# Mixture-of-experts stage of a fused transformer layer: its extra token blocks folded into two loops per expert, four weight buffers in place of three, another order of the weight transfers

## The chip, the cores and the metric

The kernel runs on one core of a Trainium2 chip. Its time is the device time of one execution in microseconds (us). The median of three runs of the kernel before is 1521.79 us (1521.5 to 1522.17). One more execution was profiled. A change under 0.2% of the time (3 us) counts as no change.

The engines are TensorE (PE, matmul), VectorE (DVE), ScalarE (ACT), GpSimd (POOL) and SyncE (SP, which here only issues transfers). Each runs its own instruction stream in order. They meet in semaphores.

## The reference

One layer for 256 prompt tokens and 64 sample tokens (T = 320), model width 2048: RMSNorm, attention and a gated convolution, output projection, and then the part that the change touches, a mixture of 32 experts with two experts per token. All in float32. Cut to what matters:

```python
gate = (g_p * top_p / sum(top_p))                     # weight of each of a token's 2 experts
expert_idx = g_idx[:, None] * 8 + top_i               # 4 groups of 8 experts
# for every expert e, on the rows xb of the tokens that chose it:
hb = silu(xb @ w_gate[e]) * (xb @ w_up[e])            # w_gate, w_up: 2048 x 512
y  = (hb @ w_down[e]) * gate                          # w_down: 512 x 2048
h  = h + segment_sum(y)                               # back to the tokens
y_prompt, y_sample = rmsnorm(h)
```

Each of the three matrices of an expert has 4 MB (4.19 million bytes), and all 32 experts are read whatever the routing is, 403 million bytes.

## The kernel before, in words

Up to about 545 us the kernel computes norms, projections, attention and the output projection with its router logits. The expert stage follows, and then a final norm of about 20 us.

**Blocks.** The tokens of an expert are handled in blocks of B = 32. With 320 tokens and two choices each, an expert has 20 tokens on average, and in these inputs one expert of the 32 has more than 32, so 33 blocks are computed: 31 experts have one block, and expert 19 has two. A table in SBUF (`tables`) holds the counts, computed by DVE, and the engines read it into registers.

**One block on PE.** `gather` picks the tokens' rows out of the normalised activations by matmul (L841); ACT copies them, `gathered_T` transposes them (L847), and ACT copies again to `xg`. `gate_or_up` multiplies by the gate matrix and then by the up matrix (L864, 16 matmuls of 32 rows each, which the profile shows as 32 records), ACT copies each result (L1191), `fold` sums four partial sums and transposes (L870). ACT computes silu (L1194), DVE multiplies (L1564) into `hT`. `down` multiplies by the down matrix (L879), ACT copies `yb` (L1234), and `combine` spreads the block's rows back over the tokens in 12 matmuls (L890), each of which DVE adds to `hreg` (L1561). `gates_T` (L852) prepares the weights that combine uses. The gather for the next expert is done between this expert's gate and up.

**PSUM banks.** combine writes its 12 pieces to the eight banks in the order `COMB_BANKS`, and an engine that wants a bank waits on `comb_added` until the addition that frees it is done. The gate result goes to bank 2, which the sixth addition frees before the change.

**Blocks beyond the first.** Expert 19's second block is `extra_blocks(e)`, a branch with its own buffers (`xx`, `hTx`, `gTx`, `yx`), which PE enters after the first block's gate and up and before its down: it computes gate and up once more with the same matrices, then down and combine, and then PE goes back for the first block's down.

**Transfers.** The weights lie in three slots of 32 KB per partition (the six 16 KB parts of `ring`): gate, up, down. SP loads expert e's gate when the gate matrix of e-1 is used, then its up, then its down (L482), each as one transfer of 4 MB, and where expert e-1 has extra blocks it waits for these as well (`extra_used`). The transfers of expert 0 are issued at the end of the output projection (L474, six of 2 MB). The gain of the final norm is loaded by POOL at `hg_ready` (1 MB).

**Names for the steps below.** U(e) is the moment at which PE is done with the up matrix of expert e-1, so that up(e) can be issued. D(e) is the start of expert e's first `down`.

## Time and profile before

| | |
|---|---|
| median of three runs | 1521.79 us |
| profiled execution, its own time | 1520.95 us |
| its span, first to last instruction | 1518.7 us |
| PE busy | 1343.1 us (88%) |
| DVE busy | 596.3 us (39%) |
| ACT busy | 347.2 us (23%) |
| granted TensorE clock, mean | 0.925 |
| moved by DMA | 473.91 MB, mean 312 GB/s |
| share of the chain that ended last: PE / DMA | 52% / 41% |

The span is 2.25 us shorter than the time of the same execution. A busy share is an average over stages with different limits: in the 40 slices of the profile the DMA engines are busy 9 tenths in nearly every slice from the 17th on, and 0 to 6 tenths in most of the slices before, while PE is busy 7 to 9 tenths in all but the first. The granted clock is in tenths of full speed (2.4 GHz), and its lower level is half of that. "Idle before, releaser" in a row is how long the engine stood still ahead of the instruction, and what released it.

### The profile page before, as it was taken

How to read it: one execution, taken by the hardware profiler on the slowest of the kernel's cores; microseconds unless marked ns; L12 is line 12 of the kernel's file. 1: busy time of each engine (PE TensorE's matmuls, PEld its weight loads, DVE VectorE, ACT ScalarE, POOL GpSimd, SP SyncE). 2: the span in 40 equal slices, each digit the busy share in tenths (PEclk: the TensorE clock that was granted, in tenths of full speed). 3: DMA queues.
4: the chain of work that ended last, by engine and by line, in shares of the span. 5: the costliest groups of instructions: out<-in, count | busy, mean ns of one | idle time of the engine just before them, and what ended most of it. 6: DMA issues, size and time to landing. Idle time of an engine off the chain costs nothing.

```text
span 1518.7 us, 22119 instructions
## 1 busy us (share of the span) xinstructions
PE 1343.1 (88%) x8510; PEld 714.1 (47%) x8511; DVE 596.3 (39%) x1183; ACT 347.2 (23%) x591; POOL 32.0 (2%) x41
## 2 busy tenths in 40 slices
PE   5999999999999999788888888888889988887885
PEld 4989999566666663232222322322323322223221
DVE  6335444044574443242243234224324422332344
ACT  5332322123453322111111111111211111111113
POOL 1000000000000000000000000000000000000000
PEclk9999999999999989999898888988989989889887
DMA  9454451023353368999999999999989999999994
GB/s 323 132 166 137 161 167 60 10 70 111 92 180 112 132 284 358 411 434 433 430 430 435 432 430 432 434 431 430 433 362 397 432 434 431 432 432 433 431 432 180
DMA packets 69607, 473.91 MB, mean 312 GB/s; under 512 B 9516, under 2 KB 46512, under 8 KB 55680
## 3 DMA queue, kind: packets, MB, share of 16 engines
q1 hardware_dynamic: 68640, 470.85, 76.0%
q0 software_dynamic: 832, 2.48, 0.5%
q8 instruction: 29, 0.48, 0.1%
q14 instruction: 10, 0.08, 0.0%
q10 hardware_dynamic: 96, 0.02, 0.0%
HBM read 469.97 MB, written 3.38 MB: 312 GB/s over the span
## 4 chain that ended last, share of the span: by engine, by line
PE 52%; DMA 41%; DVE 3%; issue 2%; ACT 1%; SPq 0%; DVEq 0%; ACTq 0%
DMA ring<-in_w_down 41%; PE ps L879 11%; PE ps L579 5%; PE ps L580 5%; PE ps L581 5%; PE ps L864 3%; PE ps L640 2%; PE ps L667 2%; PE ps L730 2%; PE ps L731 2%; PE ps L732 2%; PE ps L743 2%; PE ps L841 2%; PE ps L661 1%; PE ps L870 1%
## 5 line engine op out<-in xcount | busy, mean ns | idle before, releaser
L1561 DVE TENSOR_TENSOR hreg<-ps,hreg 128x512 f32<-128x512 f32 (+1 forms) x396 | 239.6, 679 | 290.2 <-PE ps L890 290.2
L864 PE MATMUL ps<-ring,mix 128*32 128x512 f32 x2112 | 281.6, 681 | 30.4 <-DMA ring<-in_w_up 17.9
L879 PE MATMUL ps<-ring,mix 128*32 128x512 f32 x1056 | 166.2, 787 | 60.6 <-DMA ring<-in_w_down 53.1
L890 PE MATMUL ps<-mix 32*128 32x512 f32 (+1 forms) x792 | 156.3, 612 | 26.4 <-ACT mix L1234 25.6
L1191 ACT COPY mix<-ps 128x512 f32<-128x512 f32 x66 | 70.5, 1069 | 448.3 <-PE ps L864 448.3
L864 PEld LDWEIGHTS ps<-ring,mix 128*32 128x32 f32 x2112 | 74.6, 122 | 207.8 <-issue 177.8
L579 PE MATMUL ps<-xT_hi,w_hi 128*128 128x320 f32 (+1 forms) x528 | 165.5, 313 | 4.9 <-DVE w_lo L1299 2.9
L580 PE MATMUL ps<-xT_lo,w_hi 128*128 128x320 f32 (+1 forms) x528 | 164.5, 312 | 0.0
L581 PE MATMUL ps<-xT_hi,w_lo 128*128 128x320 f32 (+1 forms) x528 | 164.4, 311 | 0.0
L1299 DVE TENSOR_TENSOR w_lo<-ring,w_hi 128x1024 fp32r<-128x1024 f32 (+1 forms) x66 | 76.7, 1205 | 105.9 <-ACT w_hi L1006 105.9
L879 PEld LDWEIGHTS ps<-ring,mix 128*32 128x32 f32 x1056 | 40.0, 138 | 160.7 <-issue 103.9
L890 PEld LDWEIGHTS ps<-mix 32*128 32x128 f32 (+1 forms) x792 | 51.3, 166 | 133.7 <-issue 68.0
L579 PEld LDWEIGHTS ps<-xT_hi,w_hi 128*128 128x128 f32 (+1 forms) x528 | 99.4, 188 | 6.2 <-issue 3.6
L841 PE MATMUL ps<-r,work 128*32 128x512 f32 (+1 forms) x840 | 101.8, 595 | 0.0
L580 PEld LDWEIGHTS ps<-xT_lo,w_hi 128*128 128x128 f32 (+1 forms) x528 | 99.6, 189 | 0.3
L581 PEld LDWEIGHTS ps<-xT_hi,w_lo 128*128 128x128 f32 (+1 forms) x528 | 99.5, 188 | 0.2
L1006 ACT CAST w_hi<-ring 128x1024 fp32r<-128x1024 f32 (+1 forms) x66 | 65.0, 1033 | 149.2 <-PE ps L581 149.2
L1564 DVE TENSOR_TENSOR mix<-mix,ps 128x128 f32<-128x128 f32 x33 | 9.5, 288 | 226.3 <-PE ps L870 216.3
L870 PEld LDWEIGHTS ps<-const,mix 128*128 128x128 f32 x528 | 63.8, 191 | 53.5 <-issue 27.7
L870 PE MATMUL ps<-const,mix 128*128 128x32 f32 x528 | 71.0, 279 | 18.2 <-ACT mix L1191 18.2
L1234 ACT COPY mix<-ps 128x512 f32<-128x512 f32 x32 | 18.8, 586 | 215.8 <-PE ps L879 215.8
L841 PEld LDWEIGHTS ps<-r,work 128*32 128x32 f32 (+1 forms) x840 | 25.6, 108 | 69.4 <-issue 68.6
(259 smaller groups left out, 1187.5 us busy)
## 6 DMA issues: line engine op xcount, KB each, us to landing
ring<-in_w_gate SPq DMA_DIRECT2D x31, 4096.0 KB, 22.1
ring<-in_w_up SPq DMA_DIRECT2D x31, 4096.0 KB, 23.7
ring<-in_w_down SPq DMA_DIRECT2D x31, 4096.0 KB, 23.7
ring<-in_w_in SPq DMA_DIRECT2D x32, 1024.0 KB, 8.2
ring<-in_w_o SPq DMA_DIRECT2D x16, 1024.0 KB, 6.8
hreg<-in_x_prompt SPq DMA_DIRECT2D x4, 1024.0 KB, 6.2
ring<-in_w_up SPq DMA_DIRECT2D x2, 2048.0 KB, 11.6
ring<-in_w_gate SPq DMA_DIRECT2D x2, 2048.0 KB, 8.2
```

Source lines behind the costliest of these rows:

```text
L579: pe.matmul(out, hi, xT_hi[:, c, :], start=c == 0, stop=False)
L580: pe.matmul(out, hi, xT_lo[:, c, :], start=False, stop=False)
L581: last = pe.matmul(out, lo, xT_hi[:, c, :], start=False, stop=c == KC - 1)
L841: last = pe.matmul(ps[B * j:B * (j + 1), bank, :], pk[0:tn, i, :], xn[0:tn, i, 4 * j:4 * j + 4, :].rearrange("t c q -> t (c q)"), start=i ...
L864: last = pe.matmul(ps[r:r + B, bank, :], x[:, k % 4, k // 4, :], w[:, k, :], start=k < 4, stop=k >= KC - 4)
L870: last = pe.matmul(ps[:, 3, 64 * c + B * m:64 * c + B * m + B], hsb[m][:, c, :], const[:, C_FOLD:C_FOLD + B], start=True, stop=True)
L879: last = pe.matmul(ps[B * j:B * (j + 1), 4, :], h[:, c, :], w[:, c, 512 * j:512 * j + 512], start=c == 0, stop=c == 3)
L890: pe.matmul(ps[0:tn, COMB_BANKS[u % 8], :], gates[r, t0:t0 + tn], rows[r, :], start=True, stop=True).then_inc(full_sem, 1)
L1006: act.copy(w_hi[:, u % 2, 8 * half:8 * half + 8, 0:width], w_raw(u, half)).then_inc(w_hi_ready, 1)
L1191: act.copy(hsb[m].rearrange("p c q -> p q c"), ps[:, bank, :].rearrange("p (q c) -> p q c", c=4)).then_inc(signal, 1)
L1299: dve.tensor_tensor(w_lo[:, u % 2, f, 0:width], w_raw(u, half), w_hi[:, u % 2, f, 0:width].bitcast(F32), ALU.subtract).then_inc(w_lo_ready, 1)
L1561: dve.tensor_tensor(h, ps[0:tn, COMB_BANKS[u % 8], :], h, ALU.add).then_inc(signal, 1)
```

## The change

1. The separate code for extra blocks is gone. For each expert PE, ACT and DVE run two loops over its blocks: the first does gate and up of every block and keeps the products in `hTs` (one place per block), the second does down and combine of every block. Before each down ACT copies the block's product from `hTs` to `hT`.
2. `gate_b`, a fourth slot of 32 KB per partition, is laid over `mix` and its neighbours, whose contents are no longer needed. Even experts take their gate matrix from the ring, odd ones from `gate_b`. Gate 1 is loaded as soon as `hg_ready` is 12.
3. SP issues, in this order: up(e) after U(e), gate(e+1), down(e). For the last two experts it is up, down, gate, up, down, and the last down comes in four pieces of 1 MB with a semaphore each.
4. A block's gates transpose waits for 5 additions of the block before it in the second loop, and its down for 6; `COMB_BANKS` is reordered. The gate matmuls wait for the seventh addition of the preceding expert's last block instead of the sixth.
5. In a block, `fold(1)` now comes ahead of `gathered_T`.
6. The gain of the final norm is loaded after the last down matrix, into the ring. The router matrix goes to `krt` and is loaded after the residual input.

The core of the diff (buffers that only move, and the semaphores' declarations, are left out):

```diff
-COMB_BANKS = (5, 6, 7, 1, 4, 2, 0, 3)
+COMB_BANKS = (5, 6, 7, 1, 0, 4, 2, 3)
...
-            sp.wait_ge(routed, 4)
-            with sp.Fori(1, NE) as e:
-                used = sp.value_load(tables[0:1, 3, bass.ds(e, 1)], min_val=1, max_val=65)
-                for m in range(3):
-                    sp.wait_ge(weights_used, e * 3 + (m + 1 - 3))
-                    sp.wait_ge(extra_used[m], used)
-                    w = a[("w_gate", "w_up", "w_down")[m]][0, bass.ds(e, 1)].rearrange("a b c -> (a b) c")
-                    sp.dma_start(ring[:, 2 * m:2 * m + 2, :].rearrange("p s n -> p (s n)"), rows_of(m, w)).then_inc(slot_full[2 * m], 16)
+            sp.wait_ge(hg_ready, 12)
+            sp.dma_start(gate_b[:, :], rows_of(0, a["w_gate"][0, 1])).then_inc(gate_b_full, 16)
+            sp.wait_ge(routed, 2)
...
+            def load_gate(e, before, dst, signal):
+                sp.wait_ge(gate_done, before)
+                sp.dma_start(dst, expert_rows("w_gate", 0, e)).then_inc(signal, 16)
+
+            def load_up(e, before):
+                sp.wait_ge(up_done, before)
...
+            before = blocks_before(1)
+            load_gate(2, before, gate_a, slot_full[0])
+            load_up(1, before)
+            load_down(1, before)
+            with sp.Fori(2, NE - 3, 2) as e:
+                before = blocks_before(e)
+                load_up(e, before)
+                load_gate(e + 1, before, gate_b[:, :], gate_b_full)
+                load_down(e, before)
+                before = blocks_before(e + 1)
+                load_up(e + 1, before)
+                load_gate(e + 2, before, gate_a, slot_full[0])
+                load_down(e + 1, before)
+
+            before = blocks_before(NE - 2)
+            load_up(NE - 2, before)
+            load_down(NE - 2, before)
+            load_gate(NE - 1, before, gate_b[:, :], gate_b_full)
+            before = blocks_before(NE - 1)
+            load_up(NE - 1, before)
+            sp.wait_ge(down_done, before)
+            for c in range(4):
+                sp.dma_start(ring[:, 4 + c // 2, D * (c % 2):D * (c % 2 + 1)],
+                             rows_of(2, a["w_down"][0, NE - 1])[:, D * c:D * (c + 1)]).then_inc(down_last[c - 1] if c else slot_full[4], 16)
...
+            def expert(e, odd):
+                first = pe.value_load(tables[0:1, 0, bass.ds(e, 1)], min_val=0, max_val=NE + 20)
+                count = pe.value_load(tables[0:1, 1, bass.ds(e, 1)], min_val=1, max_val=MAXB)
+                with pe.Fori(0, count) as k:
+                    it = first + k
+                    pe.wait_ge(xg_ready, it + 1)
+                    pe.wait_ge(comb_added, first * 12 + 7)
+                    gate_full(e, odd)
+                    gate_or_up(xg, 0, odd, 2).then_inc(gate_done, 1)
+                    pe.wait_ge(comb_added, first * 12 + 8)
+                    pe.wait_ge(pick_ready, it + 2)
+                    gather(pickr, 0, gathered)
+                    pe.wait_ge(h_copied, it * 2 + 1)
+                    pe.wait_ge(hT_ready, it + 1)
+                    fold(0).then_inc(folded, 1)
+                    matrix_full(1, e)
+                    gate_or_up(xg, 1, odd, 4).then_inc(up_done, 1)
+                    pe.wait_ge(h_copied, it * 2 + 2)
+                    pe.wait_ge(silu_ready, it + 1)
+                    fold(1).then_inc(folded, 1)
+                    pe.wait_ge(g_copied, it + 2)
+                    pe.wait_ge(comb_added, first * 12 + 12)
+                    gathered_T(gsb, 1, transposed)
+                tail = pe.value_load(tables[0:1, 2, bass.ds(e, 1)], min_val=0, max_val=16)
+                after = first + count
+                with pe.Fori(0, count) as k:
+                    it = first + k
+                    pe.wait_ge(hT_ready, after + 1)
+                    pe.wait_ge(comb_added, it * 12 + 5)
+                    pe.wait_ge(gates_ready, it + 1)
+                    gates_T(gpick, gt_full)
+                    pe.wait_ge(comb_added, it * 12 + 6)
+                    pe.wait_ge(h_picked, it + 1)
+                    down(hT, e, tail + 1).then_inc(down_done, 1)
+                    pe.wait_ge(xg_ready, after + 1)
+                    pe.wait_ge(gt_copied, it + 1)
+                    pe.wait_ge(y_copied, it + 1)
+                    pe.wait_ge(comb_added, it * 12 + 12)
+                    combine(gT, yb, comb_full, comb_added, it * 12 + 12)
...
+            with act.Fori(0, NE) as e:
...
+                after = first + count
+                with act.Fori(0, count) as k:
+                    it = first + k
+                    act.wait_ge(hT_ready, after + 1)
+                    act.copy(hT, hTs[:, bass.ds(k, 1), :].rearrange("p b q -> p (b q)")).then_inc(h_picked, 1)
...
-            pool.wait_ge(hg_ready, 12)
-            pool.dma_start(gain, a["norm_final"].rearrange("(a d) -> a d", a=1).to_broadcast([P, D])).then_inc(s_gfin, 16)
+            pool.wait_ge(down_last[2], 17)
+            pool.dma_start(gain_last, a["norm_final"].rearrange("(a d) -> a d", a=1).to_broadcast([P, D])).then_inc(s_gfin, 16)
```

How the instructions stand in a row. First SP, whose rows are the transfers, from the last of expert 0's to the loop over the experts. In the kernel before:

```order
L474 DMA ring<-in_w_down 128x4096 [waits psum_full] x2
L476 UNCONDITIONAL_BRANCH [waits routed]
L476 ISA
L477 TENSOR_LOAD tables
L477 ISA x2
L479 ISA
L482 ISA [waits extra_used0,weights_used]
L482 DMA ring<-in_w_gate 128x8192
L479 REGISTER_ALU
L482 DMA ring<-in_w_up 128x8192 [waits extra_used1,weights_used]
L482 DMA ring<-in_w_down 128x8192 [waits extra_used2,weights_used]
```

The same place in the changed kernel, to the end of the loop's first expert:

```order
L471 DMA ring<-in_w_down 128x4096 [waits psum_full] x2
L473 DMA gate_b<-in_w_gate 128x8192 [waits hg_ready]
L492 TENSOR_LOAD tables [waits routed]
L492 ISA x2
L481 DMA ring<-in_w_gate 128x8192 [waits gate_done]
L485 DMA ring<-in_w_up 128x8192 [waits up_done]
L489 DMA ring<-in_w_down 128x8192 [waits down_done]
...
L485 DMA ring<-in_w_up 128x8192 [waits up_done]
L481 ISA [waits gate_done]
L481 DMA gate_b<-in_w_gate 128x8192
L489 DMA ring<-in_w_down 128x8192 [waits down_done]
```

Gate 1 has moved ahead of the wait for the routing, and in the loop the up transfer, which waits for `up_done`, stands ahead of the next gate.

PE from the end of the up matmuls to the first down matmul, in the kernel before (L864 up, L847 gathered_T, L870 fold, L852 gates_T, L879 down; the part of the extra blocks, which is jumped over, is left out):

```order
L864 MATMUL ps<-ring,mix 32x512 x15
L944 REGISTER_ALU [waits g_copied]
L847 MATMUL ps<-const,mix 128x128 [waits comb_added]
L847 MATMUL ps<-const,mix 128x128 x3
L948 REGISTER_ALU
L870 MATMUL ps<-const,mix 128x32 [waits h_copied]
L870 MATMUL ps<-const,mix 128x32 x3
L852 MATMUL ps<-const,work 128x128 [waits gates_ready]
...
L895 COMPARE_AND_BRANCH
...
L879 MATMUL ps<-ring,mix 32x512 [waits slot_full5,slot_full4]
```

And in the changed kernel (L911 up, L917 fold, L884 gathered_T, L889 gates_T, L930 down):

```order
L911 MATMUL ps<-ring,cq 32x512 x15
L961 REGISTER_ALU
L917 MATMUL ps<-const 128x32 [waits silu_ready,h_copied]
L917 MATMUL ps<-const 128x32 x3
L965 REGISTER_ALU [waits g_copied]
L884 MATMUL ps<-const,work 128x128 [waits comb_added]
...
L947 COMPARE_AND_BRANCH
...
L889 MATMUL ps<-const,work 128x128 [waits gates_ready]
...
L900 ISA [waits h_picked,comb_added]
L930 MATMUL ps<-ring,work 32x512 [waits slot_full5,slot_full4]
```

The transposes of the gathered rows stood in the time in which ACT copies the up result, and now stand behind the fold; a loop's end and the next loop's start lie between them and gates_T, and down has a new wait, `h_picked`, for ACT's copy.

ACT in its first loop over the blocks, changed kernel (L1212 copy of the gate or up result, L1205 copy of the gathered rows, L1215 silu):

```order
L1223 ISA
L1212 ACT_TABLE_LOAD
L1212 COPY work<-ps 128x128x4 [waits gate_done]
L1204 REGISTER_ALU
L1205 COPY work<-ps 128x512 [waits gathered]
L1228 ISA
L1215 ACT_TABLE_LOAD
L1215 ACTIVATE work<-ps 128x128 [waits folded]
L1212 COPY const<-ps 128x128x4 [waits up_done]
```

Two loads of activation tables now stand inside the loop. Before, expert 0 was written out ahead of the loop with the only such load of the stage, and the loop had none.

## Rows read from the trace of the kernel before

**Rows 1.** Stretches of time: engines' busy us (instructions), granted clock, DMA share, GB/s.
```profile
567.00:575.00 8.00, 6.57 (x60) 2.17 (x52) 5.22 (x19) 1.17 (x2) 0.00 (x0) 1.00 0.17 49
575.00:668.00 93.00, 78.67 (x596) 29.69 (x592) 30.91 (x68) 19.55 (x30) 0.00 (x0) 0.94 0.99 416
668.00:1105.00 437.00, 367.97 (x2505) 126.23 (x2505) 147.90 (x315) 66.60 (x105) 0.00 (x0) 0.88 1.00 432
1131.00:1137.00 6.00, 5.54 (x51) 2.36 (x54) 1.33 (x5) 1.10 (x3) 0.00 (x0) 1.00 0.12 49
```
**Rows 2.** Timeline of PE, expert 2's down to expert 3's: start, us, what.
```profile
643.54 3.64 PE L879 MATMUL ps<-ring,mix 128*32 128x512 f32 x32
647.97 4.74 PE L890 MATMUL ps<-mix 32*128 32x512 f32 x24 [0.79 <-ACT mix L1234]
653.03 3.64 PE L864 MATMUL ps<-ring,mix 128*32 128x512 f32 x32 [0.32 <-DVE hreg L1561]
656.46 2.92 PE L841 MATMUL ps<-r,work 128*32 128x512 f32 x24
659.31 1.08 PE L870 MATMUL ps<-const,mix 128*128 128x32 f32 x8
660.32 3.64 PE L864 MATMUL ps<-ring,mix 128*32 128x512 f32 x32
663.89 0.66 PE L847 MATMUL ps<-const,mix 128*128 128x128 f32 x4
665.11 1.08 PE L870 MATMUL ps<-const,mix 128*128 128x32 f32 x8 [0.56 <-ACT mix L1191]
668.01 3.64 PE L879 MATMUL ps<-ring,mix 128*32 128x512 f32 x32 [1.37 <-DMA ring<-in_w_down]
```
**Rows 3.** Two later downs after a longer and a shorter wait.
```profile
1404.83 6.42 PE L879 MATMUL ps<-ring,mix 128*32 128x512 f32 x32 [3.38 <-DMA ring<-in_w_down]
1433.98 5.34 PE L879 MATMUL ps<-ring,mix 128*32 128x512 f32 x32 [1.54 <-DMA ring<-in_w_down]
```
**Rows 4.** Transfers whose issue ended a stretch without transfers (SP's timeline).
```profile
573.56 0.35 SPq L482 DMA_DIRECT2D ring<-in_w_gate  x1
1136.64 0.34 SPq L482 DMA_DIRECT2D ring<-in_w_gate  x1
```
**Rows 5.** One up transfer of 2 MB alone, window 505 to 520: KB, us to landing.
```profile
ring<-in_w_up SPq DMA_DIRECT2D x1, 2048.0 KB, 7.6
```
**Rows 6.** Downs of experts 18, 19 (its second block, then its first) and 22.
```profile
1105.12 6.09 PE L879 MATMUL ps<-ring,mix 128*32 128x512 f32 x32 [3.39 <-DMA ring<-in_w_down]
1145.41 3.64 PE L879 MATMUL ps<-ring,mix 128*32 128x512 f32 x32
1154.54 3.64 PE L879 MATMUL ps<-ring,mix 128*32 128x512 f32 x32
1229.99 3.64 PE L879 MATMUL ps<-ring,mix 128*32 128x512 f32 x32 [0.48 <-DMA ring<-in_w_down]
```
**Rows 7.** Around expert 0's gate: transposes, ACT's copy, gate.
```profile
568.35 0.66 PE L847 MATMUL ps<-const,mix 128*128 128x128 f32 x4 [0.71 <-ACT mix L1184]
569.04 0.59 ACT L1188 COPY mix<-ps 128x512 f32<-128x512 f32 x1 [0.75 <-PE ps L847]
569.73 3.64 PE L864 MATMUL ps<-ring,mix 128*32 128x512 f32 x32 [0.72 <-issue]
```
**Rows 8.** The gain of the final norm, in the page's list of transfers.
```profile
ckv<-in_norm_final POOLq DMA_DIRECT2D x1, 1024.0 KB, 11.9
```
**Rows 9.** ACT: the one table load of the stage, and silu in a later expert.
```profile
581.04 1.28 ACT L1194 ACT_TABLE_LOAD   x1
606.22 0.28 ACT L1194 ACTIVATE mix<-ps 128x128 f32<-128x128 f32 x1 [0.39 <-PE ps L870]
```
**Rows 10.** The last down, and the first use of the final gain.
```profile
1492.24 5.34 PE L879 MATMUL ps<-ring,mix 128*32 128x512 f32 x32 [1.66 <-DMA ring<-in_w_down]
1506.87 2.35 DVE L1656 SCALAR_TENSOR_TENSOR hreg<-hreg,small,ckv 128x2048 f32<-128x2048 f32 x1
```

More of the change, by code:

```diff
@@ L423, in late_loads @@
             sp.wait_ge(psum_full, full(f"K{H - 1}_1"))
+            sp.dma_start(gain, a["norm_ffn"].to_broadcast([P, D])).then_inc(s_gffn, 16)
+            sp.wait_ge(psum_full, full(f"PV{H - 1}"))
+            sp.wait_ge(s_stage, 64)
+            sp.wait_ge(ssq_full, 4)
+            for i, (t0, tn) in enumerate(TILES):
+                sp.dma_start(xtile[0:tn, i, :], x_src[i]).then_inc(s_xagain, 16)
             sp.dma_start(wr[:, :, 0:G], a["w_router_group"][0].rearrange("(c p) e -> p c e", p=P)).then_inc(s_router, 16)
@@ L965, in _ @@
+            for c in range(3):
+                pe.sem_inc(down_last[c], 1)
             keep_clock(3, 5)
```

345 lines of the change are left out of this document (124 added, 221 removed).

## The prediction

> **What bounds the kernel now.** I read the stretches of time first. From 668 to 1105 us the transfers run at 432 GB/s with the DMA engines' share at 1.00 [rows 1]: 15 experts in 437.1 us from expert 3's down to expert 18's [rows 2, 6], so 29.14 us per expert of three matrices, 9.71 us per matrix. There the stream of weights is the bound and nothing in this change makes it faster. The change can win only where the stream stands still, and after its end. The stretches show two such places: 567 to 575 us (49 GB/s, so 7.1 of 8 us idle) with the 93 us behind it (416 GB/s, 3.4 us idle), and 1131 to 1137 us (49 GB/s) at expert 19, the one with two blocks. For the second place the downs give the sum: from expert 18's to expert 22's, 124.87 us where four experts of 29.14 would be 116.56, so 8.3 us lost [rows 6].
>
> The timeline of PE then says how close PE is to being the bound. Where it does not wait, down to the end of up takes 4.43 (down, and ACT's copy) + 5.06 (combine, held by DVE's additions) + 3.43 (gate) + 2.85 (gather) + 1.01 (fold) + 3.57 (up) = 20.35 us, and the next down could start 2.8 us later (668.01 less its wait of 1.37, from 663.89) [rows 2]: 23.2 us, 5.9 less than the stream needs. After a wait PE is slower: the granted clock is 0.88 in the long stretch against 1.00 where PE does not wait [rows 1], and a down that takes 3.64 us takes 5.34 behind a wait of 1.54 and 6.42 behind one of 3.38 [rows 2, 3]. I take +1.7.
>
> From issue to landing a transfer costs more than its bytes. 2 MB alone took 7.6 us [rows 5], of which 4.85 are bytes at 432 GB/s, so 2.75 are not. At expert 19 the stream was empty some 2.4 us before the landing that the downs imply (1105.12 + 29.14 = 1134.3, against a stretch that is all but empty from 1131 [rows 1]), and 573.56 was followed by traffic at about 574.8 [rows 1, 4]. I take 1.0 from issue to the first byte and 2.4 from the last byte to landing, 3.4 together; bounds 2.7 and 3.7. The Trainium skill (DMA: Bandwidth & Descriptors, Anatomy of one DMA) puts the fixed cost of a DMA at about 2.0 us, most of it the receipt of the last byte. The trace shows more here; by 2.0 each of the three gaps below would be 1.4 shorter, 4 us in all, as an estimate.
>
> **PE's cycle after the change.** Gate waits for the seventh addition, not the sixth: 7.26/12 = 0.61 us more (DVE adds one piece per 0.61; combine to gate was 5.06 = six of them and the start). The time from down to the end of up is 20.96. Behind up, the fold starts 1.22 us later as before and occupies PE for 0.92 (1.08 with its end); the transposes, which stood in ACT's shadow [rows 2], now follow; transposes to the end of ACT's copy is 1.28 [rows 7]; then the new copy of hT on ACT, which no row shows. Its bounds are 0 (hidden) and the 0.59 of a copy four times as wide [rows 7]; silu on the same 128 columns takes 0.28 [rows 9], and I take 0.3. With 0.4 for semaphores and the entry to the second loop that is 4.1 in place of 2.8. The loop entry's bounds are 0 and the 0.72 that expert 0's gate waited for issue [rows 7]. So the cycle is **25.1 us**, range 24.5 to 26.5. That still fits into 29.14, but 2.3 us more of it lie on a path that decides at the places below.
>
> Is the stream still full in between? Put expert e-1's landed down at 0. The stream holds up(e), gate(e+1), down(e) and is empty at 29.1 - 2.4 = 26.7. The next up is issued at 20.96 + 1.7 = 22.7, first byte 23.7. The margin is 3.0 us, or 1.3 if the gate is slow as well. Full, at a cost of 0; if it is not, see the rivals.
>
> **The start.** The final gain (1 MB, 2.4 us of stream) leaves it: -2.4 [rows 8]. Gate 1 goes into it before the routing, 9.7 us. The stream was empty at 567, and would now be at 567 - 2.4 + 9.7 = 574.3; gate 2 is issued when expert 0's gate is done, as the gate of expert 1 was (573.56) [rows 4], so a gap of 0.5 to 0.8. Then gate 2, up 1, down 1: full to 603.9. U(2) is expert 0's end of up, 569.73 + 3.43 + 2.85 + 1.0 + 3.57 = 580.6, plus 25.1: 605.7, first byte 606.9 with the 1.2 seen here. A gap of 3.0. Together 3.8 against 7.1 + 3.4 = 10.5 before: **-6.7**, with the gain -9.1. The routing's shorter chain on DVE gains nothing (PE was still busy with its filler matmuls), and the later router load has 10 us to spare.
>
> **Expert 19.** Expert 18's down landed at 0. U(20) comes only when both blocks are done with up, and gate 21 stands behind it in SP's row. First block: end of up at 22.7. Second: fold 1.22 + 0.92, transposes to gate 1.38, gate 3.43, gather 2.85, fold 1.01, up 3.57 = 14.4 [rows 2, 7]. So U(20) = 37.1, first byte 38.1, against an empty stream at 26.7: a gap of 11.4. Then it is full to 38.1 + 29.1 = 67.2, as down 20 is issued in time: the first down at 41.2, the second 9.7 later (9.13 between the two before [rows 6], and a gates transpose), its end 54.5. The wait for five and six additions costs nothing, since four are past when combine ends and DVE needs 0.61 for each of the rest, but it does not shorten anything either. U(21) = 50.9 + 20.96 = 71.8, first byte 72.8: a second gap of 5.6. Before, the extra block's gate was used first and freed its slot at 1136.64, 31.5 us after the landing [rows 4, 6], and the gate led the queue. So 17.0 against 8.3: **+8.7**.
>
> **The end.** The last matrix would land at 1492.24 - 9.1 + 8.7 = 1491.8. But now PE is late. With expert 28's down landed at 0, eight transfers end at 77.7; D(29) = 29.1, D(30) = 29.1 + 25.1 + 1.7 = 55.9, D(31) = 81.0. So the last down starts **3.3** behind the last landing, and the four pieces overlap nothing. Because PE has not waited it is fast, 3.64 and not 5.34: **-1.7**. The final gain is loaded behind the last piece; it needs 11.9 us at worst [rows 8] and is used 14.6 - 1.7 + 3.3 = 16 us after it [rows 10]: hidden, 0.
>
> **ACT's tables.** Two loads per block, 33 blocks, 1.28 us each [rows 9]: 85 us more on ACT. The one ahead of the gate's copy runs while PE does combine. The one ahead of silu starts at about 605.8 in the terms of the rows (silu at 606.22 now), so silu ends near 607.4, and the fold that waits for it comes 4.8 us after 606.1, at 610.9. Cost 0. The Trainium skill (ScalarE: Activation LUTs, What ACT_TABLE_LOAD costs) counts 2.66 us for a switch, with a drain of 1.38 behind the 1.28. The trace shows silu 0.02 behind the load; by the page the rival with exposed tables below would cost 88 us and not 42, and its chance stays small because even 2.66 would fit under this cover.
>
> **Sum.** -2.4 - 6.7 + 8.7 + 3.3 - 1.7 = +1.2 us on the span of 1518.7: 1519.9. The profiled execution took 2.25 more than its span, 1522.2, and it lies 0.8 under the median of the runs, so **1523.0**.
>
> **Rivals.** *PE's cycle is longer (slower).* The places are U(2), U(20), U(21), D(30) and D(31): one extra us in the cycle makes the gaps 1, 1 and 2 us longer and the end 2, so 6 us per us. At 26.5, the top of my range, it is +8.4 and 1531. It decides from a cycle of 25.4 on, where the sum passes +3. For it: the new copy, two loop entries and the register loads all stand between the fold and down. Against: in the loop before, the jump over the extra part did not show. A variant is a stream that empties every time: if U comes 1 us after the margin of 3.0, each expert costs 0.5 us, since the same delay is spread over two, and 31 of them 15: about 1538. It needs a cycle beyond 28 or a slow down and a slow gate at once. *Tables exposed (slower):* if each block's load delayed a copy that PE waits for, 33 x 1.28 = 42 us, but only where PE's path decides; for all, 1565. ACT's idle time of 3 to 9 us before these copies speaks against it.
>
> *A shorter cycle (faster).* At 24.3 (the hT copy and the loop entry hidden, the transposes not) it is -4.8: 1518.2. *The double expert costs what it did (faster).* If the second gap of 5.6 is not there, because PE is ahead by more than I count, 1517.4; with the first gap short too, 1514.3. That needs expert 19 to start before its down of 18 landed, which the row of SP doesn't allow. *The change does only what the start shows:* with the double expert and the end as before, 1523.0 - 8.7 - 3.3 + 1.7 = 1512.7; I see no reason for that in the rows, but it is the lower bound.
>
> **How the numbers follow.** Chances: forecast within 3 us (which is 0.2%, what a measurement can tell) 0.38; longer cycle 0.25, a stream that empties 0.06, tables 0.03, so slower 0.34; shorter cycle 0.15, the double expert 0.10, only the start 0.03, so faster 0.28. The cycle's range of 24.5 to 26.5 alone gives 1519.4 to 1531.4; the latency's bounds of 2.7 to 3.7 move the gaps' sum by -2 to +1, and whether downs and gates are slow or fast at experts 19 and 29 by 3 either way. The range is 1514 to 1532; the forecast's own is 1520 to 1526.
>
> **What would show it.** Per expert 29.14 us between landed downs in the long stretch, at 432 GB/s. Gate 1's transfer issued near 545.5, no stretch of 7 us without traffic at 567. A stretch without traffic of some 11 us after expert 18's down, and one of 5 to 6 about 30 us later. Gate 5.67 us after combine's start, down about 4.1 after the end of up where nothing else is late. A last down without a DMA wait ahead of it, 3.64 us long. I am wrong if the stream stays full at expert 19, or if it shows gaps at every expert.

## The result, and the profile after the change

| | before | after |
|---|---|---|
| median | 1521.64 us (1521.5 to 1522.17, 4 runs) | 1539.57 us (1536.62 to 1542.97, 4 runs) |
| profiled execution: time / span | 1520.95 / 1518.7 us | 1537.64 / 1535.8 us |

The ratio after/before is 1.0119, 95% interval 1.0105 to 1.0132: slower by 18 us, 16.6 above the forecast of 1523.0 and 7.6 above the range's upper end. The page of the kernel after: busy time, and the chain that ended last.

```profile
PE 1322.5 (86%) x8482; PEld 703.6 (46%) x8483; DVE 597.9 (39%) x1176; ACT 440.1 (29%) x687; POOL 31.9 (2%) x41
PE 57%; DMA 34%; DVE 3%; issue 3%; ACT 2%; DVEq 0%; SPq 0%; ACTq 0%
```

The share of DMA in the chain fell from 41% to 34% and PE's rose from 52% to 57%: PE decides more of the time. Stretches of the kernel after, against [rows 1] (columns as there):

```profile
567.00:575.00 8.00, 6.27 (x44) 2.37 (x48) 1.44 (x4) 2.19 (x3) 0.00 (x0) 0.79 0.78 334
604.00:609.00 5.00, 4.84 (x44) 1.91 (x40) 0.00 (x0) 2.24 (x4) 0.00 (x0) 1.00 0.29 121
670.00:1105.00 435.00, 354.36 (x2490) 120.83 (x2490) 146.47 (x306) 107.86 (x146) 0.00 (x0) 0.90 1.00 429
1138.00:1152.00 14.00, 13.06 (x100) 4.15 (x98) 1.24 (x5) 5.14 (x7) 0.00 (x0) 0.88 0.00 0
1182.00:1190.00 8.00, 7.14 (x64) 2.51 (x56) 0.00 (x0) 3.95 (x5) 0.00 (x0) 1.00 0.04 16
```

Each gap is where it was forecast, and each is larger. The old one at 567 has shrunk (334 GB/s in place of 49), but 573 to 575 still carries only 25 GB/s: gate 2 waits for expert 0's gate, which took 5.34 and not the 3.64 of [rows 7] (the window, and the gate on PE's timeline):

```profile
573.00:575.00 2.00, 2.00 (x24) 0.86 (x20) 0.00 (x0) 0.32 (x1) 0.00 (x0) 0.93 0.08 25
569.29 5.34 PE L911 MATMUL ps<-ring,cq 128*32 128x512 f32 x32 [1.73 <-issue]
```

The new one at 604 cost 5.1 us where 3.0 were forecast (3.6 of them in this window, by its 121 GB/s against 432, the rest until up 2's first byte behind it). Behind expert 18 nothing moves for 14 us (11.4 forecast), and 30 us later for 8 more (5.6 forecast). In the last three gaps PE is over 85% busy: the transfers wait for PE.

SP's timeline of the kernel after shows what ended the gaps, against [rows 4], where it was a gate:

```profile
609.05 0.35 SPq L485 DMA_DIRECT2D ring<-in_w_up  x1
609.61 0.34 SPq L481 DMA_DIRECT2D gate_b<-in_w_gate  x1
1152.11 0.33 SPq L485 DMA_DIRECT2D ring<-in_w_up  x1
1152.64 0.33 SPq L481 DMA_DIRECT2D gate_b<-in_w_gate  x1
1189.20 0.34 SPq L485 DMA_DIRECT2D ring<-in_w_up  x1
```

An up ends each of these three gaps, and 0.5 us behind it comes a gate whose slot had long been free: it stood in SP's row behind the up that waited.

PE's timeline over one cycle of the kernel after, from expert 0's down to expert 1's, in which PE waits for no transfer, against [rows 2]:

```profile
585.77 3.64 PE L930 MATMUL ps<-ring,work 128*32 128x512 f32 x32 [0.30 <-ACT work L1237]
590.30 4.76 PE L941 MATMUL ps<-krt,const 32*128 32x512 f32 x24 [0.88 <-ACT krt L1241]
596.22 5.34 PE L911 MATMUL ps<-gate_b,cq 128*32 128x512 f32 x32 [1.16 <-DVE hreg L1564]
601.37 2.90 PE L878 MATMUL ps<-r,work 128*32 128x512 f32 x24
604.19 1.08 PE L917 MATMUL ps<-const,work 128*128 128x32 f32 x8
605.20 3.64 PE L911 MATMUL ps<-ring,cq 128*32 128x512 f32 x32
609.99 1.08 PE L917 MATMUL ps<-const 128*128 128x32 f32 x8 [1.15 <-ACT const L1212]
610.90 0.64 PE L884 MATMUL ps<-const,work 128*128 128x128 f32 x4
611.76 0.64 PE L889 MATMUL ps<-const,work 128*128 128x128 f32 x3 [0.23 <-DVE work L1568]
612.71 3.64 PE L930 MATMUL ps<-ring,work 128*32 128x512 f32 x32 [0.31 <-ACT work L1237]
```

The cycle is 26.9 us, not 25.1. The way from the end of up (608.8) to down is 3.9, as forecast (4.1). Combine to gate is 5.9 (forecast 5.67), but the gate takes 5.34 where I had 3.64 from [rows 2]; over the next such gate, from 623.58 to 628.95, the granted clock is 0.68. PE stood idle for 1.16 ahead of it, and not 0.32 as there. For even experts combine to gate is 6.34 with 1.58 idle, and the cycle 27.4 to 27.9 where no transfer is waited for.

Three of the periods between downs are 31.3 us and not 29.14, two in the long stretch (from 669.96 and 963.44) and one from 1396.86. The first of them on PE's timeline:

```profile
669.96 6.46 PE L930 MATMUL ps<-ring,work 128*32 128x512 f32 x32 [2.59 <-DMA ring<-in_w_down]
683.67 6.43 PE L911 MATMUL ps<-ring,cq 128*32 128x512 f32 x32 [1.58 <-DVE hreg L1564]
693.75 3.64 PE L911 MATMUL ps<-ring,cq 128*32 128x512 f32 x32
701.25 3.64 PE L930 MATMUL ps<-ring,work 128*32 128x512 f32 x32 [0.30 <-ACT work L1237]
```

Down and gate both run slow, up ends at 697.4, which is 27.4 behind the landed down, and the stream is empty at 26.7 by the forecast's own working: the "slow down and slow gate at once" of the rival of a stream that empties. The end, PE, POOL and DVE, against [rows 10]:

```profile
1494.41 5.34 PE L911 MATMUL ps<-gate_b,cq 128*32 128x512 f32 x32 [1.07 <-DVE hreg L1564]
1510.90 3.64 PE L930 MATMUL ps<-ring,work 128*32 128x512 f32 x32 [0.30 <-ACT work L1237]
1505.18 0.60 POOL L580 DMA_DIRECT2D ring<-in_norm_final  x1 [1084.61 <-DMA ring<-in_w_down]
1523.93 2.35 DVE L1635 SCALAR_TENSOR_TENSOR hreg<-hreg,small,ring 128x2048 f32<-128x2048 f32 x1
```

The last piece landed at 1505.18 (POOL was released then), the last down started 5.7 behind it (3.3 forecast) and took 3.64 as forecast. The final gain is used 18.7 us after its issue: hidden.

The profiled executions by segments, the times of expert n's down being D(n); a loss is the segment less 29.14 us per expert. The kernels to the right are experiments below.

| | before | after | e2 | e9 | e10 | e11 |
|---|---|---|---|---|---|---|
| D(3) at | 668.0 | 670.0 | 667.3 | 675.7 | 670.5 | 672.1 |
| lost D(3) to D(18) | 0.0 | 3.2 | 0.2 | 2.2 | -0.7 | -3.5 |
| lost D(18) to D(22), with expert 19 | 8.3 | 23.3 | 18.5 | 16.5 | 18.2 | 10.0 |
| lost D(22) to D(29) | 0.0 | 2.1 | -2.6 | 0.8 | -10.5 | -10.8 |
| D(29) to D(31) | 58.3 | 54.8 | 54.2 | 52.2 | 54.1 | 56.1 |
| D(31) to the end | 26.5 | 24.9 | 24.9 | 26.6 | 24.9 | 26.6 |

In e10 and e11 down 29 stands ahead of gate 30 in the queue, which alone takes 9.7 off the fourth line.

Against the forecast, after is +1.4 at D(3) (668.0 - 9.1 and one more matrix ahead of it, 9.7, is 668.6), +3.2 in the long stretch, +6.3 at expert 19, +2.1 behind expert 22, +2.9 from D(29) to D(31) (51.9 forecast) and +0.1 behind it: 16.0, and 1519.9 + 16.0 = 1535.9 for a span of 1535.8.

### The profile page after: what moved, and what is told of

Its sections match the earlier page's. It is cut to its first block, busy times and chain, and to the rows that moved or that the text cites. A ratio compares the mean times of both kernels' runs of the same rounds, so it can differ in the third digit from the quotient of the medians.

```text
span 1535.8 us, 23172 instructions
## 1 busy us (share of the span) xinstructions
PE 1322.5 (86%) x8482; PEld 703.6 (46%) x8483; DVE 597.9 (39%) x1176; ACT 440.1 (29%) x687; POOL 31.9 (2%) x41
## 4 chain that ended last, share of the span: by engine, by line
PE 57%; DMA 34%; DVE 3%; issue 3%; ACT 2%; DVEq 0%; SPq 0%; ACTq 0%
DMA ring<-in_w_down 33%; PE ps L930 11%; PE ps L911 7%; PE ps L615 5%; PE ps L616 5%; PE ps L617 5%; PE ps L878 2%; PE ps L676 2%; PE ps L703 2%; PE ps L766 2%; PE ps L767 2%; PE ps L768 2%; PE ps L779 2%; PE ps L917 2%; DVE hreg L1564 1%
## 5 line engine op out<-in xcount | busy, mean ns | idle before, releaser
L911 PE MATMUL ps<-ring,cq 128*32 128x512 f32 x1568 | 195.4, 642 | 25.3 <-DVE hreg L1564 23.5
L930 PE MATMUL ps<-ring,work 128*32 128x512 f32 x1056 | 163.6, 776 | 51.6 <-DMA ring<-in_w_down 48.6
L941 PE MATMUL ps<-krt,const 32*128 32x512 f32 (+1 forms) x792 | 157.0, 613 | 29.5 <-ACT krt L1241 29.5
L911 PEld LDWEIGHTS ps<-ring,cq 128*32 128x32 f32 x1568 | 53.3, 116 | 137.0 <-issue 135.3
L941 PEld LDWEIGHTS ps<-krt,const 32*128 32x128 f32 (+1 forms) x792 | 48.9, 166 | 140.3 <-issue 75.5
L1212 ACT COPY work<-ps 128x512 f32<-128x512 f32 x33 | 36.1, 1093 | 269.0 <-PE ps L911 269.0
L930 PEld LDWEIGHTS ps<-ring,work 128*32 128x32 f32 x1056 | 40.1, 137 | 147.9 <-issue 95.8
L911 PE MATMUL ps<-gate_b,cq 128*32 128x512 f32 x544 | 74.5, 697 | 18.2 <-DVE hreg L1564 17.3
L917 PE MATMUL ps<-const 128*128 128x32 f32 x264 | 35.6, 279 | 37.8 <-ACT const L1212 37.8
L917 PEld LDWEIGHTS ps<-const 128*128 128x128 f32 x264 | 31.9, 191 | 67.8 <-ACT const L1212 67.8
## 6 DMA issues: line engine op xcount, KB each, us to landing
ring<-in_w_down SPq DMA_DIRECT2D x30, 4096.0 KB, 23.3
ring<-in_w_gate SPq DMA_DIRECT2D x15, 4096.0 KB, 23.4
ring<-in_w_up SPq DMA_DIRECT2D x2, 2048.0 KB, 10.5
```

The lines of the kernel that those rows point to most:

```text
L911: last = pe.matmul(ps[r:r + B, bank, :], x[:, k % 4, k // 4, :], w[:, k, :], start=k < 4, stop=k >= KC - 4)
L917: last = pe.matmul(ps[:, 3, 64 * c + B * m:64 * c + B * m + B], hsb[m][:, c, :], const[:, C_FOLD:C_FOLD + B], start=True, stop=True)
L930: last = pe.matmul(ps[B * j:B * (j + 1), 4, :], h[:, B * c:B * (c + 1)], w[:, c, 512 * j:512 * j + 512], start=c == 0, stop=c == 3)
L941: pe.matmul(ps[0:tn, COMB_BANKS[u % 8], :], gates[r, t0:t0 + tn], rows[r, :], start=True, stop=True).then_inc(full_sem, 1)
L1212: act.copy(hsb[m].rearrange("p c q -> p q c"), ps[:, bank, :].rearrange("p (q c) -> p q c", c=4)).then_inc(signal, 1)
```

## The experiments

Theory A: PE's cycle is 27 to 28 us, and the places where the stream waits for PE turn that into time; SP's order (the free gate behind the waiting up) makes each place dearer. Rivals: the double expert alone; the seventh addition; the tables.

**e1, the gate needs only the fifth addition.** A cheaper cause of the idle time ahead of the gate.

```
-COMB_BANKS = (5, 6, 7, 1, 0, 4, 2, 3)      gate waits for comb_added first * 12 + 7
+COMB_BANKS = (5, 6, 7, 1, 2, 0, 4, 3)      gate waits for comb_added first * 12 + 5
```

(In exchange gates_T waits for the sixth addition and down for the seventh, one more each.)

> The changed kernel with another bank order: the gate result goes to the bank that the fifth addition frees, not the seventh, so gate follows combine after about 0.1 to 0.5 us and not 1.1 (1.6 in even experts). Theory A (PE's cycle decides at the start, at expert 19 and at the end, and the short idle ahead of gate costs the slow clock too: gate 5.34 instead of 3.64): cycle shorter by 0.6 to 1.0 for the wait and by up to 1.7 for the clock, six times: 1539.6 - 6 to - 14, so 1526 to 1534. Theory B (the loss is in the order of the transfers alone): 1537 or more.

Measured: 1541.27 us (1540.95 to 1544.21), ratio 1.0133 (1.0116 to 1.015). No gain; it was expected at 1526 to 1534. PE's timeline of e1 at the first such gate, and DVE's with the twelve additions before it:

```profile
599.86 5.34 PE L911 MATMUL ps<-gate_b,cq 128*32 128x512 f32 x32 [1.14 <-DVE hreg L1564]
595.12 7.26 DVE L1564 TENSOR_TENSOR hreg<-ps,hreg 128x512 f32<-128x512 f32 x12 [4.11 <-PE ps L941]
```

Five additions at 0.605 each end near 598.2, and gate starts 1.6 us later. The idle time is as long as with seven, though the profile still names DVE as releaser. With two additions less to wait for, nothing changed, so in this kernel the addition does not end the wait; something later does, which e7 looks for, and the releaser in the row is only the last semaphore that the view could name.

**e2, the next gate ahead of up in SP's loop.**

```
-                load_up(e, before)
                 load_gate(e + 1, before, gate_b[:, :], gate_b_full)
+                load_up(e, before)
```

(and so for the odd expert.)

> The changed kernel with SP's order next gate, up, down in the loop (the end of the program as it is). Theory A: the stream stands still at expert 19 because gate 21 is queued behind up 20; with gate 21 issued at the end of the second block's gate (7.7 us before its up) the gaps of 14.6 and 8 become together about 15, and the gap of 5 at 604 goes: about 12 us less, 1526 to 1530. Theory B (the stream's gaps are not what sets the end, PE's own cycle is): less than 4 us, 1536 or more.

Measured: 1523.57 us (1521.99 to 1524.74, 10 runs), ratio 1.0008 (0.9998 to 1.0018): 16 us less than after (12 expected), and no different from before. SP's timeline of e2 at the double expert:

```profile
1139.07 0.33 SPq L481 DMA_DIRECT2D gate_b<-in_w_gate  x1
1146.35 0.34 SPq L485 DMA_DIRECT2D ring<-in_w_up  x1
1163.48 0.33 SPq L489 DMA_DIRECT2D ring<-in_w_down  x1
```

The gate leads and fills the stream for 9.7 us while PE does gather and up. The table shows the gain in every segment but the last (3.0 in the long one, 4.8 at expert 19, 4.7 behind it); the gap at 604 is gone. PE's cycle is no shorter (26.9 from D(0) to D(1)): the order alone keeps the stream fed. Its largest cost left over before is still expert 19, 18.5 against 8.3, now in three gaps of 9, 4.5 and 3 us.

**e3 and e4, one block per expert, in after and in before.** One line on DVE sets the number of further blocks to zero.

```
             link(dve.tensor_reduce(extra, cmp, AX, ALU.add))
+            link(dve.tensor_scalar(extra, extra, 0.0, None, ALU.mult))
```

> The changed kernel without expert 19's second block (its tokens beyond 32 are added into another expert's rows). Theory A: the gaps at expert 19 cost 22.6 us here, so 1517 plus or minus 3, and the difference to the same edit in the kernel before is 2 to 6 us. Theory B (each expert costs more, everywhere): 1528 or more, difference 12 or more.

> The kernel before, also without expert 19's second block. Both theories: the 8.3 us that the downs of experts 18 to 22 show go, 1513 to 1514. It is the other half of the comparison with the one-block form of the changed kernel.

Measured: e3 1518.87 us (1512.8 to 1520.64, 10 runs), ratio 0.9973 (0.996 to 0.9986); e4 1514.93 us (1513.49 to 1516.35), ratio 0.9957 (0.994 to 0.9974). Both kernels leave out the second block. The double block costs 20.7 us in after and 6.7 in before: about 14 of the 18 us are made at expert 19, give or take 3 by the intervals; the table's 23.3 against 8.3 says 15. The remaining 4 are the long stretch, which shows in e3 as in after (3.15 lost from D(3) to D(18)), and the late end, less the start's gain.

**e5, the transposes ahead of the second fold again.**

```
+                    pe.wait_ge(g_copied, it + 2)
+                    pe.wait_ge(comb_added, first * 12 + 12)
+                    gathered_T(gsb, 1, transposed)
                     pe.wait_ge(h_copied, it * 2 + 2)
```

(and taken out behind the fold.)

> The kernel after, with PE's transposes of the gathered block (0.64 us) ahead of the second fold again, where they stood before, in the shadow of ACT's copy (fold idles 1.15 for it). Theory A (the loss is PE's own row of work, 6 us of time per us of its cycle): the way from the end of up to down goes from 4.0 to 3.5 (not more, since the gates' transposes and ACT's copy of hT then end at nearly the same time), so 0.4 to 0.5 per cycle, 2 to 4 us in all: 1535.5 to 1537.5 against 1539.6. Rival B (the order of the transfers alone sets the gaps, PE's cycle hardly counts): no change, 1539.6 within 1.5.

Measured: 1532.08 us median, but 1530.48 to 1541.86 over five runs; ratio 1.0069 (1.0049 to 1.009). Four runs lie within 2 us, 7 below after; the fifth is the profiled one, so its trace shows none of the gain: there expert 0's down took 5.34 instead of 3.64, and the gate behind it 6.48. It does show the way from the end of up to down, 3.5 in place of 3.9. A gain of 7 us is more than six times 0.4. Rival B is unlikely by the four runs, but no trace shows their gain; why they are so good is open.

**e6, no table loads in the loop.** One Silu on a spare column stands ahead of it.

```
+            act.activation(small[:, 63:64], eps_col, ACT.Silu)
             act.wait_ge(routed, 2)
```

> The kernel after with one Silu on a spare column ahead of ACT's loop, so that the loop needs no table loads (66 fewer, 85 us of ACT's time). Theory A (both loads of a block lie behind work of PE): no change, 1539.6 within 1.5. Rival T (the load ahead of silu or of the gate's copy delays a copy that PE waits for): up to 1.28 per cycle at the places where PE decides, 6 places at least: 1532 or less.

Measured: 1536.57 us (1531.63 to 1539.14), ratio 1.0092 (1.0065 to 1.012), which overlaps after's interval. PE's cycle is 26.90 from D(0) to D(1) against 26.94, and expert 19 costs 22.7 against 23.3. The loads are hidden, as forecast. ACT's timeline of the kernel after, against [rows 9]:

```profile
659.91 1.28 ACT L1215 ACT_TABLE_LOAD   x1
661.20 0.28 ACT L1215 ACTIVATE work<-ps 128x128 f32<-128x128 f32 x1
663.88 1.02 ACT L1212 COPY const<-ps 128x512 f32<-128x512 f32 x1 [2.41 <-PE ps L911]
```

Silu starts 0.01 behind the load, and ACT then has 2.4 us until up is done. The drain of 1.38 us that the Trainium skill (ScalarE: Activation LUTs, What ACT_TABLE_LOAD costs) adds to a load does not appear here.

**e7, e3 with straight code on PE.**

```
-                with pe.Fori(0, count) as k:
-                    it = first + k
+                first = it = e
```

(both loops; the loads of first and count go.)

> The kernel after with one block per expert as in e3 (the second block of expert 19 is left out and its tokens go to another expert's rows), and PE's two inner loops over blocks replaced by straight code for one block: no loads of first and count, no loop ends. To be compared with e3's 1518.9. Theory L (the idle time of 1.1 and 1.6 us between combine and gate is PE's sequencer at the loops' ends and register loads, and gate is slow, 5.34 for 3.64, because the clock falls in that idle time): idle before gate under 0.6 for odd experts, gate 3.5 to 3.8, cycle near 25, last down 3 to 4 behind the last landing in place of 5.7, gap at 604 near 3: 1512 to 1516. Rival S (the wait is for DVE's seventh addition, as the profile's releaser says, or for another engine's loop): idle unchanged, 1518.9 within 2.

Measured: 1507.96 us (1506.84 to 1512.12), ratio 0.9913 (0.9893 to 0.9933), below the 1512 to 1516 expected. Like e3 it leaves out the second block. PE's timeline of e7:

```profile
588.61 4.74 PE L941 MATMUL ps<-krt,const 32*128 32x512 f32 x24 [0.90 <-ACT krt L1236]
594.15 3.64 PE L911 MATMUL ps<-gate_b,cq 128*32 128x512 f32 x32 [0.80 <-DVE hreg L1559]
608.94 5.32 PE L930 MATMUL ps<-ring,work 128*32 128x512 f32 x32 [0.33 <-ACT work L1232]
```

Combine to gate is 5.54 (5.65 for even experts), idle 0.80 and 0.91, and the cycle from the down at 584.07 to that at 608.94 is 24.9. What is left of the idle time agrees with the seventh addition alone (0.32 before, plus 0.61): by DVE's timeline gate now starts 0.1 to 0.2 us behind the end of that addition, where in after it starts 0.4 behind it, 0.9 for even experts. With a fast gate the forecast's 25.1 holds. So the inner loop's end and its loads are worth 0.3 us, 0.7 with the outer loop's. The idle time was forecast under 0.6 and is 0.8, for which that addition is enough. The medians of e7 and e3 differ by 10.9 us, the profiled executions only by 3.0 (e7's is the slowest of its four), and all of it was made before D(0), at 584.07 against 587.07. From D(0) to D(3) e7 is 0.3 ahead, and behind it not at all. So the trace shows the shorter cycle, and no trace shows what the shorter cycle gained in time: the 10.9 us are not explained.

**e8, three fillers behind combine, and e12, one.**

```
                     combine(gT, yb, comb_full, comb_added, it * 12 + 12)
+                    pe.wait_ge(comb_added, it * 12 + 17)
+                    keep_clock(3, 0)
```

> The kernel after with a wait for the fifth addition behind combine and three filler matmuls (3 x 0.21 us, into the bank that it frees) at the end of PE's second loop, so that PE works while its sequencer goes through the loop's end. Theory C (gate is slow because the granted clock falls in the idle time, 0.68 in that stretch): gate 3.5 to 3.9 in the places where PE decides, cycle 1 to 1.6 shorter, 6 us per us: 1530 to 1535. Rival D (gate is slow for another reason, such as the transfers that write beside it; or the fall comes all the same, from the 0.6 of waiting ahead of the fillers): gate 5.3, the cycle the same or 0.3 longer, 1539 to 1542.

Measured: 1546.98 us (1542.41 to 1551.05), ratio 1.017 (1.0138 to 1.0202): 7 slower than after. PE's timeline of e8:

```profile
593.44 4.76 PE L941 MATMUL ps<-krt,const 32*128 32x512 f32 x24 [0.88 <-ACT krt L1243]
598.13 2.84 PE L855 MATMUL ps<-const 128*128 128x512 f32 x6
600.90 3.64 PE L911 MATMUL ps<-gate_b,cq 128*32 128x512 f32 x32
```

Theory C is right on the gate: with no idle time ahead of it, it takes 3.64 in all 31 cycles (14 of 31 take 5.00 or more in after). Part of the low clock comes back elsewhere: 23 of the 33 downs take 5.0 us or more, 17 in after. Summed up, what gates and ups take above 3.64 each falls from 29.7 us to 1.7, and what downs take above it rises from 43.5 to 51.4. And a filler takes 0.95 us, not the 0.21 that I wrote, so three of them use up what the clock gives back (cycle 26.8), and in the double expert they stand twice. One filler:

> e8 with one filler matmul in place of three. e8 showed the gates at 3.64 us, but its three fillers took 2.84 us, more than the idle time of 1.1 to 1.6 that they filled, and the double expert has them twice more. One takes 0.95. Theory C (the clock falls in the idle time at the loop's end): gate 3.64 in most places and cycle 25.9 to 26.6 in place of 26.9 to 28.1, so 1530 to 1536. Rival D (one filler of 0.95 with idle time on both sides holds no clock): gates 5.3 again, 1538 to 1543.

Measured: 1538.28 us (1533.87 to 1541.04), ratio 1.0105 (1.0073 to 1.0137). 3 of 31 gates are slow and the first cycle is 25.8, yet expert 19 costs 23.0, as in after, and the time moves by no more than the runs spread. Two of the three slow gates stand where PE decides (627.11, and expert 20's at 1180.09, 5.27), and the first down of expert 19 takes 5.16 there. Inconclusive as a remedy.

**e9, PE's first block straight, a loop only for more.**

```
+                one(first, first)
+                count = pe.value_load(tables[0:1, 1, bass.ds(e, 1)], min_val=1, max_val=MAXB)
+                with pe.If(count > 1):
+                    with pe.Fori(1, count) as k:
+                        one(first + k, first)
```

(`one` is the body of the first loop, `two` that of the second, treated alike.)

> The kernel after, all blocks computed, but PE's first block of an expert is straight code and a loop follows only where there are more (first is loaded once per pair of experts, count behind up). Theory L (the prediction's cycle of 25.1 us failed only by the loops' ends on PE and the low clock that they bring): cycle 24.8 to 25.3 where PE does not wait, and with it the places as predicted: gap at 604 of 2 to 3, last down 3 to 4 behind the last landing, expert 19 about 17 us lost in place of 22.6; the prediction's sum for this cycle was 1523.0, so 1521 to 1527. Rival O (the places are set by the other engines' loops or by the order of the transfers, and e7's gain belongs to one block alone): 1530 or more.

Measured: 1536.17 us (1533.82 to 1537.82), ratio 1.0101 (1.0075 to 1.0126). As a time this is a miss (1521 to 1527 expected; 1530 or more was the rival's). Its downs at expert 19, PE's timeline of e9:

```profile
1115.01 5.75 PE L930 MATMUL ps<-ring,work 128*32 128x512 f32 x32 [2.49 <-DMA ring<-in_w_down]
1156.31 3.64 PE L930 MATMUL ps<-ring,work 128*32 128x512 f32 x32 [0.30 <-ACT work L1246]
1166.08 3.64 PE L930 MATMUL ps<-ring,work 128*32 128x512 f32 x32
1191.27 5.17 PE L930 MATMUL ps<-ring,work 128*32 128x512 f32 x32
1248.02 5.80 PE L930 MATMUL ps<-ring,work 128*32 128x512 f32 x32 [2.63 <-DMA ring<-in_w_down]
```

41.3, 9.8 and 25.2 us, where the forecast had 41.2, 9.7 and 25.1, and after 45.5, 9.8 and 27.5. The loss from D(18) to D(22) is 16.5 against the forecast's 17.0. One trace could be luck, but this place repeats: in the four kernels with loops and up ahead of gate the loss is 22.7 to 23.4 (after, e1, e5, e6). Expert 19's first gate takes 4.96 to 6.59 and expert 20's 5.34 to 5.43 in all six with loops and no filler (e2 and e10 too), and 3.64 to 3.78 in both with straight code (e9, e11). Expert 20's gate, PE's timelines of after and of e9:

```profile
1176.42 5.43 PE L911 MATMUL ps<-ring,cq 128*32 128x512 f32 x32 [1.56 <-DVE hreg L1564]
1176.28 3.64 PE L911 MATMUL ps<-ring,cq 128*32 128x512 f32 x32 [0.92 <-DVE hreg L1573]
```

In the segments e9 gains 6.8 here, 1.0 in the long stretch, 1.3 and 2.6 behind it, and loses 1.7 by a slow last down (5.32). It loses 5.7 by D(3) (675.7 against 670.0). Its execution was late before the code that e9 changes: the transfers of expert 0 are issued at 546.08, 3.6 later than in after, and expert 0's gate starts 2.9 later (572.16 against 569.29). Expert 0's down then takes 6.25 (3.64 in after) with a break of 0.26 that waits for nothing shown, the two gates behind it are slow in spite of the straight code (600.23 and 627.18, 5.34 each), and up 2 is issued at 613.06 (609.05). Why the first pass is slow was not tested.

**e10, e2 with the last gates behind down.** With the gate ahead, down 29 lands 9.7 us later than it need, and PE has two cycles left for five transfers.

```
-            with sp.Fori(2, NE - 3, 2) as e:
+            with sp.Fori(2, NE - 7, 2) as e:
+            for e in range(NE - 6, NE - 1):
+                load_up(e, before)
+                load_down(e, before)
+                load_gate(e + 1, ...)
```

> e2 (in the loop the next gate ahead of up), with the last experts' transfers in another order: from expert 26 on the next gate stands behind down, so that down 26 to down 30 come 9.7 us earlier in the stream than with the gate ahead. Theory E (at the end PE has two cycles of 27 to do in the five transfers behind down 29, 48.6 us, and is 5.2 late; with five experts to catch up in it is not): the last down 1 to 2 behind the last landing, 3 to 5 us less than e2's 1523.6: 1518.5 to 1520.5. Rival P (PE is behind all the way from expert 19, or the gates now come late): 1522.5 or more.

Measured: 1515.59 us (1508.18 to 1517.29, 10 runs), ratio 0.9956 (0.9941 to 0.9971): 8 us less than e2, more than the 3 to 5 expected. PE's and POOL's timelines of e10 at the end:

```profile
1489.37 3.64 PE L934 MATMUL ps<-ring,work 128*32 128x512 f32 x32 [0.30 <-ACT work L1241]
1492.04 0.60 POOL L584 DMA_DIRECT2D ring<-in_norm_final  x1 [1069.48 <-DMA ring<-in_w_down]
```

The last down starts 2.7 ahead of the last piece's landing, not 1 to 2 behind it: since down waits for its first piece only, PE and the stream end together. In e2 it started 5.2 behind.

**e11, e10, e9 and e5 in one.**

> e10, e9 and e5 in one: next gate ahead of up in the loop, the last experts' gates behind down, PE's first block as straight code, transposes ahead of the second fold. With a cycle of 24.5 to 25 in place of 27 to 28 expert 19 should lose about 8 us less than e2's 16 (four cycles and the double block stand in that place): 1510 to 1514, below before's 1521.6. Rival P (the gains overlap: where the stream never stands still PE's cycle is worth nothing, and expert 19 is set by its 46 us of two blocks): 1517 to 1520.

Measured: 1510.27 us (1509.31 to 1514.04, 5 runs), ratio 0.9933 (0.9911 to 0.9954): 10.5 us faster than before and 29 faster than after. Expert 19 costs 10.0 us against e2's 18.5 and e10's 18.2, as expected. From D(3) to D(18) the kernel is ahead of 29.14 per expert by 3.5, only because D(3) was late.

## Why the prediction was wrong

- **Start.** Gate 1 was issued at 544.97, and of the gap at 567 the part to 573 closed. Up 2 was issued at 609.05 and not 605.7: 1.3 us because expert 0's gate was slow, 1.8 by the longer cycle, 0.2 for the issue. The slow gate delayed the stream's own work too, so the new gap is 5.1 and not 3.0.
- **The failed step: "So the cycle is 25.1 us".** Its terms were gate's 3.43 from [rows 2] and +0.61 for the seventh addition. The addition was right (e7: combine to gate 5.54, first cycle 24.9). What I left out stands on PE's sequencer between combine and gate, the end of one loop over blocks and the loads and start of the next: 0.3 and 0.7 us by after against e7. At expert 0's gate it shows alone: 1.73 idle with the loop, 0.96 without (e7). And I took the gate as fast wherever PE waits for no transfer, from one row of 3.64 [rows 2]. In after it takes 5.00 to 6.47 us in 14 of 31 cycles, those at the start, at expert 19 and at the end among them: 1.7 in most such cycles (1.4 to 2.8), the larger term. The trace of before already had it: 15 of its 31 gates behind a combine took 5.2 to 5.34, hidden under the stream. One row was read as the rule. Over the whole kernel the loop's idle time is not needed for a slow gate: behind 0.32 to 0.55 idle (before) 15 of 31 are slow, behind 0.8 to 0.9 (e9, e7) 7 and 9, behind 1.1 to 1.6 between 8 and 15 (14 in after, 8 in e3, 15 in e10), behind none (e8) 0. At expert 19, where it counts, the gates were slow with the loops and fast without them, and the loss fell to 16.5.
- **The rival "PE's cycle is longer"** was the right mechanism. Its top of 26.5 was too low: I had searched loop entries between fold and down, where they cost nothing that shows, and argued from the jump over the extra part in the loop before. At 26.9 to 27.4 its own rate of 6 us per us gives 1533.8 to 1536.8; the measured 1539.6 also has the long stretch in it. The rival of a stream that empties names 1538, the nearest to the measured time, but by luck: it counts 15 us over 31 experts, and here three experts cost 5.
- **"Full, at a cost of 0"** for the long stretch failed: twice in the 15 experts to D(18) and once behind expert 22 down and gate met the low clock together, and the period was 31.3. The stretches lost 3.2 and 2.1 us.
- **Latency of a transfer.** 3.4 us from issue to landing beyond the bytes was too much, and its bounds of 2.7 to 3.7 too. The up that ends the gap at 1152 met an empty queue and landed 12.3 us after its issue, 2.6 more than the 9.71 of its bytes; the one at 1189 took 12.2, as did the gate at 1136.64 in before. The excess of 0.8 sits behind the last byte, so the first gap at expert 19, which is counted from a landed down, should have been 0.8 us shorter than the working has, and the margin in the long stretch 0.8 wider. That is against the direction of the miss. Issues with KB and us to landing, in after, window 1151 to 1165:

```profile
ring<-in_w_up SPq DMA_DIRECT2D x1, 4096.0 KB, 12.3
```

- **Expert 19.** 23.3 lost, 17.0 forecast; with the cycle as forecast (e9) it is 16.5. The up that holds the gate behind it was named and priced; e2 shows that it is worth 16 us over the whole kernel.
- **End.** The last down was 5.7 behind the last landing and not 3.3; the fast last down and the hidden gain were right.
- **Tables.** Right: cost nothing that can be measured (e6).

Open are what decides whether a gate meets the low clock (e7's at 594.15 is fast behind 0.80 idle, e9's at 600.23 slow behind 0.82), where the 10.9 us between e3 and e7 come from, and why kernels in which PE decides spread by up to 11 us between executions (e5). Part of that is older than the expert stage: in the profiled executions of after and its variants expert 0's transfers are issued between 542.5 and 546.1. And no single run corrects the cycle alone and reaches the forecast: e9 gives the forecast's loss at expert 19, and its time is 1536.

## What to carry to other kernels

Where a queue issues in order, put the transfer whose slot is free first ahead of the one that must wait for the slowest engine; with four slots instead of three, that order alone was worth 16 us, and with it the changed kernel only equals the kernel before (e2); it takes the other order at the end and straight code on PE to win 10 (e11). When an engine is 4 us from being the bound, price what lies between its instructions (the ends of loops, register loads), count over all its cycles how often a matmul meets the lower clock instead of taking one row, then ask at which places its cycle is paid for more than once. Near the end of a stream change the order again, so that the engine's last cycles and the last transfers end together.

## What the runs showed of the hardware

- A loop's end with two register loads and the next loop's start cost PE 0.3 us beyond a wait that was there anyway, 0.7 with the outer loop's branch; the profile books it to the last semaphore before it.
- The same 32 records of gate took 3.64 us each time with no idle time ahead (e8: 31 of 31, granted clock 1.00 over the one at 600.90) and 4.9 us or more in 3 to 15 of 31 cases behind 0.32 to 1.6 us of it, with no trend in the length of the idle time (3 in e12, 7 in e9, 8 in e3, 14 in after, 15 in before). The granted clock over one of 5.34 is 0.68 (596.22 to 601.56 in after) and over one of 6.43 it is 0.56 (683.67 to 690.10): most of its length at the lower of the two levels. With the gates fast, more downs took 5.0 us or more (23 against 17), and the mean clock rose from 0.932 to 0.945.
- A transfer of 4 MB into an empty queue brought its first packet 0.96 us after its issue (1152.11 to 1153.07 in after) and landed 12.2 to 12.3 us after it.
- A filler matmul of 128x512 in f32 took 0.95 us (2.84 for three): one of them is most of the 1.1 to 1.6 us of idle time that it should fill.
